# Splitting loaded weights in whole chunks of 128x1024 instead of blocks of 128x512, with a ring of two chunks

## The reference

```
c_act = silu(c);  mod = c_act @ ada_w + ada_b            # 6 x 2048 values
u = rms_norm(h) * (1 + sc1) + sh1
h = h + g1 * hybrid_mixer(u, w_in, ..., w_out)           # u @ w_in, attentions, o @ w_out
u = rms_norm(h) * (1 + sc2) + sh2
h = h + g2 * (silu(u @ w_gate) * (u @ w_up)) @ w_down
h = rms_norm(h)
# second block, layer 0 (pooling) and layer 1 (block attention)
u = h @ w_in2[i];  ...;  y = mixed @ w_out2[i];  h = layer_norm(ALPHA * h + y)
k, v = h @ w_kv        # between the two layers
```

## Time and profile before

| | us |
|---|---|
| median of 3 runs | 2327.52 (2325.42 to 2329.5) |
| span of the profiled execution | 2324.9 |
| the profiled execution's own time beside its span | only the span is given; the median lies 2.6 above it |
| PE matmuls busy | 2105.9 (91%) |
| DVE busy | 1503.5 (65%) |
| ACT busy | 1063.4 (46%) |
| POOL busy | 117.8 (5%) |
| chain of work that ended last | PE 75%, DVE 11%, issue 6% |

### The profile page before, as it was taken

One profiled execution on the slowest core, in us unless ns is written; L12 is line 12 of the kernel. 1 busy time (PEld: TensorE's weight loads), 2 busy tenths in 40 slices (PEclk: granted clock), 3 DMA queues, 4 the chain that ended last, 5 costly groups with the idle time before them and its releaser, 6 DMA issues.

```text
span 2324.9 us, 29571 instructions
## 1 busy us (share of the span) xinstructions
PE 2105.9 (91%) x9820; PEld 1731.4 (74%) x9820; DVE 1503.5 (65%) x2632; ACT 1063.4 (46%) x1931; POOL 117.8 (5%) x188
## 2 busy tenths in 40 slices
PE   6928999998798999999999999799799699999797
PEld 4817888776576887888888888588578578888675
DVE  5988888656898877555555556755345755555466
ACT  3414444466334544445544554455334445555542
POOL 2000000221003000000000000100000300000000
PEclk9958999999899999999999999899899899999998
DMA  9986998523796997666656665466526356664462
GB/s 299 387 297 230 359 320 312 172 80 89 278 335 203 293 292 244 199 191 190 189 188 194 190 189 186 132 196 193 166 78 226 109 168 194 190 197 138 154 218 99
DMA packets 321589, 486.09 MB, mean 209 GB/s; under 512 B 33696, under 2 KB 145536, under 8 KB 320064
## 3 DMA queue, kind: packets, MB, share of 16 engines
q1 hardware_dynamic: 318704, 468.63, 62.6%
q0 software_dynamic: 2768, 15.98, 1.9%
HBM read 465.13 MB, written 2.10 MB: 201 GB/s over the span
## 4 chain that ended last, share of the span: by engine, by line
PE 75%; DVE 11%; issue 6%; SPq 3%; DMA 2%; ACT 2%; POOL 0%; DVEq 0%; POOLq 0%; ACTq 0%
PE ps L444 23%; PE ps L446 23%; PE ps L445 23%; DVE ada_acc L385 4%; SPq L812 3%; DVE w_lo L370 3%; PE ps L483 1%; PE ps L696 1%; PE ps L659 1%; ACT w_hi L338 1%; DMA raw<-in_w_mem_kv 1%; PE ps L1311 1%; PE ps L643 1%; DVE evac L551 1%; DMA raw<-in_w_out 1%
## 5 line engine op out<-in xcount | busy, mean ns | idle before, releaser
L370 DVE TENSOR_TENSOR w_lo<-raw,w_hi 128x512 fp32r<-128x512 f32 (+1 forms) x1328 | 919.1, 703 | 628.4 <-ACT w_hi L338 626.2
L338 ACT ACTIVATE w_hi<-raw 128x512 fp32r<-128x512 f32 (+1 forms) x1328 | 829.4, 629 | 1004.4 <-PE ps L446 893.0
L444 PE MATMUL ps<-w_hi,actT 128*128 128x512 f32 (+1 forms) x2304 | 915.1, 397 | 60.3 <-DVE actT L558 24.4
L446 PE MATMUL ps<-w_hi,actT 128*128 128x512 f32 (+1 forms) x2304 | 901.7, 391 | 0.0
L445 PE MATMUL ps<-w_lo,actT 128*128 128x512 f32 (+1 forms) x2304 | 901.2, 391 | 0.0
L444 PEld LDWEIGHTS ps<-w_hi,actT 128*128 128x128 f32 x2304 | 437.4, 190 | 162.2 <-DVE actT L558 27.9
L446 PEld LDWEIGHTS ps<-w_hi,actT 128*128 128x128 f32 x2304 | 437.0, 190 | 92.1
L445 PEld LDWEIGHTS ps<-w_lo,actT 128*128 128x128 f32 x2304 | 438.3, 190 | 88.5 <-issue 1.4
L385 DVE SCALAR_TENSOR_TENSOR ada_acc<-raw,c_col,ada_acc 128x512 f32<-128x512 f32 x360 | 271.7, 755 | 11.7 <-DMA raw<-in_ada_w 2.3
L444 PE MATMUL ps<-w_hi,hidT 128*128 128x512 f32 x352 | 137.7, 391 | 2.8 <-DVE w_lo L370 2.8
L446 PE MATMUL ps<-w_hi,hidT 128*128 128x512 f32 x352 | 137.0, 389 | 0.0
(11 more groups left out here) (212 smaller groups left out, 1056.6 us busy)
## 6 DMA issues: line engine op xcount, KB each, us to landing
raw<-in_w_in SPq DMA_DIRECT2D x216, 512.0 KB, 4.1
raw<-in_ada_w SPq DMA_DIRECT2D x192, 512.0 KB, 5.6
raw<-in_w_out SPq DMA_DIRECT2D x96, 512.0 KB, 4.9
raw<-in_ffn_w_gate SPq DMA_DIRECT2D x176, 256.0 KB, 2.9
raw<-in_ffn_w_up SPq DMA_DIRECT2D x176, 256.0 KB, 3.1
raw<-in_ffn_w_down SPq DMA_DIRECT2D x88, 512.0 KB, 4.1
raw<-in_w_kv_shared SPq DMA_DIRECT2D x48, 512.0 KB, 3.7
raw<-in_w_mem_kv SPq DMA_DIRECT2D x32, 512.0 KB, 8.8
```

The costliest lines, as they stand in the source:

```text
L338: act.activation(w_hi[:, g, 0:w], raw[:, slot, b, 0:w], ACT.Copy).then_inc(hi_ready, 1)
L370: nc.vector.tensor_tensor(w_lo[:, g, 0:w], raw[:, slot, b, 0:w], w_hi[:, g, 0:w].bitcast(f32), ALU.subtract).then_inc(blocks_read, 1)
L444: nc.tensor.matmul(o, hi, w_hi[:, g, 0:w], start=(k == 0), stop=False)
L446: last = nc.tensor.matmul(o, lo, w_hi[:, g, 0:w], start=False, stop=(k == nk - 1))
```

## The change

RING stays 8; HILO = 4 becomes HI = 2. A place of the rings is now a whole chunk, so their bytes are the same. ACT rounds a chunk with one instruction and DVE takes its difference with one; PE waits once per chunk and gives its place back after both blocks. The hooks and leads of both k of a chunk stand ahead of its rounding and of its difference. The count `blocks_read` is replaced by `lo_ready` (a difference per chunk) and `ada_step` (each ada step), and the slots are counted in chunks; `slot_free` finds for SP which of the two a slot's last reader raises.

```diff
-RING, HILO = 8, 4
+RING, HI = 8, 2
-        k += _nk * len(_kind)
-        g += _nk * ("w" in _kind)
+        k += _nk // 2 * len(_kind)
+        g += _nk // 2 * ("w" in _kind)
...
-        w_hi = at("w_hi", [P, HILO, NC], f32r, r_hilo)
-        w_lo = at("w_lo", [P, HILO, NC], f32r, r_hilo + HILO * NC * 4)
+        w_lo = at("w_lo", [P, HI, 2, NC], f32r, r_hilo + HI * 2 * NC * 4)
+        w_hi = at("w_hi", [P, HI, 2, NC], f32r, r_hilo)
...
+        def slot_of(st, j, off):
+            return (st.start[0] + st.local[j][0] + off) % RING
+
+        loaded = "".join(k for st in STAGES for _ in range(st.bodies)
+                         for kd, nk in st.panels for k in kd * (nk // 2))
+
+        def slot_free(sp, st, p, first, j, off):
+
+            per = st.per[0]
+            n = st.start[0] + st.local[j][0] + off - RING + (0 if first else per)
+            if n < 0:
+                return
+            if loaded[n] == "w":
+                done, each = loaded[:n + 1].count("w"), st.per[1]
+                sp.wait_ge(lo_ready, done if first else done - each + p * each)
+            else:
+                done, each = 2 * loaded[:n + 1].count("a"), 2 * (per - st.per[1])
+                sp.wait_ge(ada_step, done if first else done - each + p * each)
...
-                        sp.wait_ge(blocks_read, pl.kb + off + 2)
+                        slot_free(sp, st, p, first, j, off)
...
# stage_split_hi (ACT)
-                            act.wait_ge(parts_used, pl.gb + k + 1)
-                            g = (st.local[j][1] + k) % HILO
-                            act.activation(w_hi[:, g, 0:w], raw[:, slot, b, 0:w], ACT.Copy).then_inc(hi_ready, 1)
+                        act.wait_ge(parts_used, pl.gb + ch + 1)
+                        g = (st.local[j][1] + ch) % HI
+                        act.activation(w_hi[:, g, :, 0:w], raw[:, slot, :, 0:w], ACT.Copy).then_inc(hi_ready, 1)
...
# stage_split_lo (DVE)
-                                dve.wait_ge(hi_ready, pl.gb + k + 1)
-                                g = (st.local[j][1] + k) % HILO
-                                nc.vector.tensor_tensor(w_lo[:, g, 0:w], raw[:, slot, b, 0:w],
-                                                        w_hi[:, g, 0:w].bitcast(f32),
-                                                        ALU.subtract).then_inc(blocks_read, 1)
+                            dve.wait_ge(hi_ready, pl.gb + ch + 1)
+                            g = (st.local[j][1] + ch) % HI
+                            nc.vector.tensor_tensor(w_lo[:, g, :, 0:w], raw[:, slot, :, 0:w],
+                                                    w_hi[:, g, :, 0:w].bitcast(f32),
+                                                    ALU.subtract).then_inc(lo_ready, 1)
...
-                                    dve.wait_ge(blocks_read, 2 * RING + pl.kb + off + b - (1 if b else
-                                                1 + 2 * (len(kinds[j]) - 1)) + 1)
+                                dve.wait_ge(ada_step, pl.an * KD + k)
...
# ada_sum (PE)
-            pe.wait_ge(blocks_read, 2 * RING + pl.kb + nk * len(kind))
+            pe.wait_ge(ada_step, pl.an * KD + KD)
...
# stage_matmuls (PE)
-                            pe.wait_ge(blocks_read, 2 * RING + pl.kb + off + b + 1)
-                            g = (st.local[j][1] + k) % HILO
+                            if b == 0:
+                                pe.wait_ge(lo_ready, pl.gb + ch + 1)
+                            g = (st.local[j][1] + ch) % HI
...
-                            last.then_inc(parts_used, 1)
+                        last.then_inc(parts_used, 1)
...
-            eng.wait_ge(parts_used, HILO + pl.gb + st.panels[j][1])
+            eng.wait_ge(parts_used, HI + pl.gb + st.panels[j][1] // 2)
...
-            pe.sem_inc(parts_used, HILO)
+            pe.sem_inc(parts_used, HI)
...
-            dve.sem_inc(blocks_read, 2 * RING)
```

More of the change, by code:

```diff
@@ L271, in body @@
                 for j in range(len(st.panels)):
-                    pl = place(st, p, j)
                     for kind, ch, off in chunks(st, j):
-                        slot = ((st.start[0] + st.local[j][0] + off) // 2) % RING
-                        sp.wait_ge(blocks_read, pl.kb + off + 2)
+                        slot = slot_of(st, j, off)
+                        slot_free(sp, st, p, first, j, off)
                         if kind == "w":
@@ L293, in program @@
                 for kind, ch, off in chunks(st, j):
-                    s = ((st.start[0] + st.local[j][0] + off) // 2) % RING
+                    s = slot_of(st, j, off)
                     cnt[s] += 32 if st.name.startswith("gu") and kind == "w" else 16
@@ L325, in body @@
                             continue
-                        for b in range(2):
-                            k = 2 * ch + b
+                        for k in (2 * ch, 2 * ch + 1):
                             if hooks and k in hooks and not (first and j == 0):
@@ new lines, in body @@
+                        wait_chunk(dve, st, p, j, idx)
+                        for k in (2 * ch, 2 * ch + 1):
+                            if k == 0:
+                                nc.vector.tensor_scalar(acc, raw[:, slot, 0, :], c_col[:, 0:1], None,
+                                                        ALU.mult).then_inc(ada_step, 1)
+                            else:
+                                dve.wait_ge(ada_step, pl.an * KD + k)
+                                nc.vector.scalar_tensor_tensor(acc, raw[:, slot, k % 2, :], c_col[:, k:k + 1], acc,
+                                                               ALU.mult, ALU.add).then_inc(ada_step, 1)
@@ L443, in body @@
                                 o = ps[:, bank + t, 0:w]
-                                nc.tensor.matmul(o, hi, w_hi[:, g, 0:w], start=(k == 0), stop=False)
-                                nc.tensor.matmul(o, hi, w_lo[:, g, 0:w], start=False, stop=False)
-                                last = nc.tensor.matmul(o, lo, w_hi[:, g, 0:w], start=False, stop=(k == nk - 1))
-                            last.then_inc(parts_used, 1)
+                                nc.tensor.matmul(o, hi, w_hi[:, g, b, 0:w], start=(k == 0), stop=False)
+                                nc.tensor.matmul(o, hi, w_lo[:, g, b, 0:w], start=False, stop=False)
+                                last = nc.tensor.matmul(o, lo, w_hi[:, g, b, 0:w], start=False, stop=(k == nk - 1))
+                        last.then_inc(parts_used, 1)
             run_bodies(pe, st, body)
```

26 lines of the change are left out of this document (9 added, 17 removed).

## The result

| | before | after |
|---|---|---|
| median of the runs | 2327.99 us (4 runs, 2325.42 to 2329.5) | 2389.64 us (4 runs, 2380.64 to 2396.16) |
| span of the profiled execution | 2324.9 us | 2394.4 us |
| PE waiting for w_lo | 20.4 us, 20 times | 42.7 us, 37 times |

The ratio is 1.0274, 95% interval 1.0252 to 1.0296. The forecast was 2366, in a range of 2346 to 2402: slower as forecast, by 62 us instead of 38.

What follows compares the result with a forecast made beforehand. PE, busy 91% of the span, was taken as the bound, with ring reserve falling from 2.5 us to nil. Hooks, leads, quiet chunks and stage starts summed to 38.2 us on 2327.5, giving 2366 us, range 2346 to 2402.

Steps and rivals of the forecast that it cites:

- down0, down1, out0, out1: DVE hooks delay PE by their length less 1.58 us: eight of 1.07 us (8.6) and six of 0.94 (+5.6).
- Quiet chunks: Chunks without hooks: path of 2.68 to 2.74 us against 2.72, 0 to 6 us over some 560 chunks, 3 taken.
- rival 1: Closed path of a quiet chunk is longer than a chunk; 0.1 us more gives 28 us on top, 2394; chance 0.18.
- down2: Hook with statistics takes 3.85 us, costing 2.27 in each of three; less the 1.3 paid before, +5.5 us.
- wout: With ada sums, take_rows and f: stall plus slow-clock matmuls make a panel 27.9 us, 2.0 more, three times, +6.
- rival 2: Clock falls after each new stall, not only those over 2 us: +25 us, 2391; chance 0.1.
- win_end: Lost reserve behind cmp_positions adds 1.3 us, and with the stage's small hooks +2 us.
- gu0: up_mul takes about 0.76 us where DVE has 0.13 in the four panels with ada: +2.5 us.
- ACT's hooks: Two copies, about 1 us, fit into ACT's free 1.74 us of a chunk and cost nothing.
- Leads: Stage starts with modulated input: 1.8 us each for u1 and u2, +0.5 and -1 for h0 and h1, sum +3.
- The transfers ... cost 0: Loads, SP's waits and their order stay as before and cost 0; a late load would show the prediction wrong.
- Rivals 3 and 4: 3: hooks absorbed, time stays at 2327, chance 0.06. 4: DVE's shorter work gains 11 us in ada panels, 2316, chance 0.06.

Runs made afterwards that it cites:

- Four places: After with four chunk places in the rings instead of two, paid for with four raw slots instead of eight: 2417.09 us, ratio to before 1.0397.
- parts under 1.58 us: After with DVE's multiplies, additions and statistics of the down and out stages queued one chunk apart: 2368.79 us, ratio to before 1.0177.
- a shorter path: After with DVE's difference as two 512-column instructions, PE waiting for each block: 2356.31 us, ratio to before 1.0128.
- the second profile of after: After, unchanged, run once more: 2388.01 us, ratio to before 1.0272.

## Why the prediction was right, and where its sizes were off

Over the chunks, the two profiles differ by 62.5 us; another 7 lie between stages and ahead of the first. I sorted the chunks by the starts of their first matmuls.

- **The mechanism** held: a reserve of 2.5 us falls to nothing, and DVE's pieces that it had hidden fall on PE. Four places bring the time of quiet and hook chunks back, parts under 1.58 us do so for the hooks, a shorter path for the quiet ones.
- **Instruction costs** were right to 0.02 us. The reason given for ACT's lower end, "PSUM no quicker than SBUF", runs the wrong way, and the rows don't bear it out: a 128x512 copy on ACT took 0.59 us from PSUM and 0.63 from SBUF, as the long ones took 1.02 and 1.06.
- **down0, down1, out0, out1**: forecast 1.07 and 0.94 a hook; measured 0.78 to 0.85 and 0.13 to 0.17 behind it, about 0.98. 14 hooks make 13.7 us against 14.2.
- **Quiet chunks**, forecast 3 us: the term that failed most. 569 chunks that differ from before by under 0.2 us hold 18.7 us; of this 3 to 4.5 follow longer stalls, and 14 to 16 are the closed path. The step that failed is "the restart of PE ... so 0.16": it was read where PE had waited 1.35 us. In the quiet path it is 0.23. With the hand-over of 0.20 to 0.26 the path is then 2.74 to 2.80 instead of 2.68 to 2.74, and the mean excess of 0.025 to 0.03 us a chunk, shared by two, stands for 2.77 to 2.78. This is rival 1, given 0.18, with its mechanism and half of its size.
- **down2**, forecast 5.5: measured 8.71. The hook chunks are 2.11 to 2.15 us over 2.72, 0.61 in before: 4.6 of the 5.5. In two of the three, matmuls at the clock's lower level follow, as here, behind an idle PE of 1.93 us:

```profile
1493.34 0.50 PE L457 MATMUL ps<-w_hi,hidT 128*128 128x512 f32 x1 [1.93 <-DVE w_lo L384]
...
1494.65 0.63 PE L459 MATMUL ps<-w_hi,hidT 128*128 128x512 f32 x1
1495.08 0.63 PE L457 MATMUL ps<-w_hi,hidT 128*128 128x512 f32 x1
```

  The chunk behind costs 1.58 and 1.41 us there instead of 0.13. The prediction had this in wout and forgot it in down2, though its own 2.27 was long enough. Behind the stall of 0.60 shown above the matmuls stayed at 0.39 to 0.40, and the chunk behind each of the 14 hooks of down0, down1, out0 and out1 is at most 0.17 too long, where the lower level cost over 1.2: rival 2 falls as it was put, "after each new stall".
- **The clock** is the term that the sum lacks. Of the 7968 weight matmuls, 84 are shown with 0.55 to 0.70 us in before and 147 in after. At the lower level they follow each other after 0.43 us instead of 0.23, so 63 more make some 12.6 us, an estimate, of which wout may hide a part. By stage they are 24 more in win_end, 18 in wout, 14 in down2, 6 in memkv, 6 in in0 and 5 in kv. The prediction kept the lower level for stalls "of over 2 us". In after it also followed idle times of 1.48, 1.93, 1.97 and 1.98 us. How often it comes differs between executions: the second profile of after has 124.
- **wout**: forecast 6 as three panels of 2.0; measured 7.31, with 1.8, 1.1 and 4.4 in the three, so the sum agrees better than its parts. The middle one took 27.85 us against 27.9 worked out, but 26.72 in before against 25.9. **gu0**: 2.5 and 1.8 for its lead; measured 5.49, of which the lead has 2.37.
- **ACT's hooks**, forecast 0: right for the copies alone, 1.2 us short for the two table loads of in1 shown above.
- **Leads**: the rounds of u1 went from 3.42 to 3.78 as worked out (differences at 206.92 and 210.70), and win's lead cost 1.83 against 1.8. For h0 and h1 the forecast of +0.5 and -1 was wrong: +2.34 and +1.44. The rounds ahead of the long waits for GpSimd grew by 0.44 to 0.59 each, and the waits did not shrink by as much; 6 and 5 more matmuls at the lower level are 1.2 and 1.0 us of the two.
- **win_end**, forecast 2: 5.4, in the second profile of after 5.7. Most of this is the clock: 24 more slow matmuls at 0.20 us are 4.8 us. Behind cmp_positions, where the prediction looked for the loss, PE's wait grew from 1.20 to 1.56 us only. The first of the slow matmuls stand in the first chunk of the stage, ahead of its hooks, behind an idle time of 1.48 us (0.94 in before, and no slow matmuls there):

```profile
383.99 0.47 PE L457 MATMUL ps<-w_hi,actT 128*128 128x512 f32 x1 [1.48 <-DVE w_lo L384]
...
385.22 0.63 PE L459 MATMUL ps<-w_hi,actT 128*128 128x512 f32 x1
```

- **"The transfers ... cost 0"** was wrong for memkv, where a late load, one of its own signs of being wrong, did appear: +5.0, in the second profile of after +2.9. ACT waits up to 4.3 us for a load there (3.3 in before), and in the first profile PE then waits 1.97 us and runs seven slow matmuls, which the second has not. The second half of a raw slot is read 1.6 us after a place came free in before, and the whole of it 0.23 + 1.06 + 1.22 = 2.5 us after it in after, so each load is asked for later in a stage where loads are what is late. That four slots cost memkv 22 us shows how little there is to spare; the 1 us itself was not tested alone.
- **Rivals 3 and 4** fell: no stage is shorter by DVE's saved work.

The profiled spans differ by 69.5 us where the steps gave 38.2. What was off there: quiet chunks +11 to +13, memkv +5, win_end +3.4, down2 +3.2, h0 and h1 +4.3, wout and gu0 with its lead +2.5, the table loads +1, the attention stretch +4.5 (open); small terms of the other sign take off some 4, above all the lead of out1 at -2.0, where before has 9 slow matmuls and after none. So the time fell into the range with the mechanism of ring and hooks right, while the clock, some 12 us by the estimate above, was in the sum with 1.6 us a panel of wout alone. The medians differ by 62, since the profiled execution of after was among its slower ones.

## What to carry to other kernels

When an edit makes pieces larger in the same memory, count the places, not the bytes: follow the material once round the ring (free, first engine, second engine, consumer) and set it against what the consumer does meanwhile. If the difference is nil, every piece of other work longer than the idle time of a chunk falls on the consumer; measure hand-overs in the quiet path itself, as a few hundredths recur hundreds of times. Expect more than the stall itself where it is long: here matmuls at the clock's lower level followed some stalls of 1.5 us and more. Pieces queued between pipeline steps should each be shorter than that idle time; here the better kernel became 0.2% faster by it (0.1 to 0.3%).

## What was not expected of the hardware

- Two 128x512 roundings in a row on ACT take 1.15 us, one of 128x1024 takes 1.06: fusing saves 0.09 us, while the first half is ready 0.43 us later. On DVE a pair takes 1.29 and one long difference 1.22 to 1.23.
- PE took up new material 0.23 us after DVE's end in a quiet chunk, 0.16 where it had waited.
- Of the three stalls of down2, an idle time of 1.96 us was followed by matmuls at full speed and one of 1.93 us by matmuls at 0.63 us, the clock's lower level: the idle time alone did not decide it. In the second profile of the same kernel one of the three was followed by them instead of two.
- Four raw slots of 512 KB in place of eight are not enough where PE's weight chunks and ada chunks come together: win fell from 312 to 274 GB/s and lost 24 us; with weight chunks alone (194 GB/s in in1) four are enough.
- A table load on ACT took 1.28 us. Ahead of ACT's two copies it cost PE 0.6 us where the ring had no reserve, and nothing where it had 2.5 us.
